# Spare blocks' expert weights: conditional plain transfers from SyncE in place of indirect loads from GpSimd

## What is computed

```python
gates = jnp.einsum('tk,tke->te', w, jax.nn.one_hot(idx, N_EXPERTS, dtype=F32))
def expert(acc, p):
    e_g, e_u, e_d, g = p                       # (1024,256), (1024,256), (256,1024), (T,)
    a = jax.nn.silu(t @ e_g) * (t @ e_u)
    return acc + g[:, None] * (a @ e_d).astype(F32), None
routed, _ = lax.scan(expert, jnp.zeros(t.shape, F32), (wg, wu, wd, gates.T))
```

## Time and profile before

| | us |
|---|---|
| median of 3 runs (lowest to highest) | 1770.37 (1769.48 to 1772.65) |
| profiled execution, span | 1780.7 |
| PE matmul busy | 1625.1 |
| DVE busy | 960.2 |
| POOL busy | 697.5 |
| ACT busy | 238.9 |

### The profile page before, as it was taken

How to read it: one execution, slowest core, us unless ns; L and a number is a source line. 1 busy time by engine, 2 the same in 40 slices (tenths; PEclk the granted TensorE clock), 3 DMA queues, 4 the chain that set the end, 5 groups by cost and what they waited for, 6 DMA issues and landing times.

```text
span 1780.7 us, 27338 instructions
## 1 busy us (share of the span) xinstructions
PE 1625.1 (91%) x10621; PEld 911.0 (51%) x10621; DVE 960.2 (54%) x2404; ACT 238.9 (13%) x607; POOL 697.5 (39%) x755
## 2 busy tenths in 40 slices
PE   7898998999799999999879989899999999999894
PEld 4674774444344444444367547644444444444443
DVE  3887467544345544444469663764444444444346
ACT  3223331000002100000031333100000000000001
POOL 1306006554454454544102240355445454545420
PEclk9998999999999999999989979999999999999997
DMA  9668475999999999999965765499999999999973
GB/s 324 226 238 289 147 281 220 413 372 339 403 410 384 366 403 409 401 373 383 370 232 189 261 241 215 179 365 407 384 383 414 402 389 394 414 387 388 397 280 150
DMA packets 185918, 588.83 MB, mean 331 GB/s; under 512 B 67705, under 2 KB 85837, under 8 KB 131902
## 3 DMA queue, kind: packets, MB, share of 16 engines
q1 hardware_dynamic: 115504, 506.99, 72.8%
q0 software_dynamic: 67232, 79.73, 13.0%
q10 hardware_dynamic: 3054, 0.38, 0.2%
HBM read 775.22 MB, written 56.95 MB: 467 GB/s over the span
## 4 chain that ended last, share of the span: by engine, by line
PE 60%; another core or an unknown queue 19%; DVE 9%; issue 4%; DMA 4%; ACT 3%; SPq 0%; POOL 0%; DVEq 0%; ACTq 0%; POOLq 0%
PE ps L1447 29%; PE ps L1460 9%; PE ps L1149 4%; PE ps L980 4%; PE ps L1295 3%; PE ps L1036 2%; ACT scratch L1745 2%; DMA raw<-in_exp_w_up,idx_w 2%; PE ps L1013 1%; PE ps L1044 1%; DMA ypart<-yrows_k 1%; PE ps L1438 1%; DVE scratch L2125 1%; DMA yrows_k<-ytok,idx_y 1%
## 5 line engine op out<-in xcount | busy, mean ns | idle before, releaser
L1447 PE MATMUL ps<-raw,xTs 128*64 128x256 f32 x6144 | 746.0, 394 | 5.3 <-DMA raw<-in_exp_w_up,idx_w 3.6
L1447 PEld LDWEIGHTS ps<-raw,xTs 128*64 128x64 f32 x6144 | 416.9, 136 | 267.1 <-issue 12.0
L927 POOL DMA_INDIRECT yrows_k<-ytok,idx_y x192 | 197.1, 1027 | 501.1 <-DVE ytok L2131 472.2
L1460 PE MATMUL ps<-dn,scratch 128*64 128x512 f32 x1536 | 364.7, 595 | 18.9 <-issue 17.2
L2246 DVE STREAM_TRANSPOSE xTs<-xg 64x256 f32<-64x256 f32 x768 | 335.7, 437 | 8.9 <-DMA xg<-hrows,idx_x 1.1
L2125 DVE TENSOR_TENSOR scratch<-scratch,ps 128x128 f32<-128x128 f32 x192 | 55.2, 287 | 434.7 <-ACT scratch L1745 361.9
L920 POOL DMA_INDIRECT xg<-hrows,idx_x x192 | 199.0, 1036 | 103.6 <-issue 57.1
L2131 DVE COPY ytok<-ps 128x512 f32<-128x512 f32 x192 | 132.3, 689 | 168.8 <-PE ps L1460 145.0
L1745 ACT ACTIVATE scratch<-ps 128x128 f32<-128x128 f32 x192 | 53.2, 277 | 1122.2 <-PE ps L1447 692.9
L1460 PEld LDWEIGHTS ps<-dn,scratch 128*64 128x64 f32 x1536 | 107.9, 136 | 167.3 <-issue 134.7
L980 PEld LDWEIGHTS ps<-cst,scratch 128*128 128x128 f32 x224 | 31.0, 141 | 216.0 <-issue 111.6
(11 more groups left out here) (394 smaller groups left out, 1296.3 us busy)
## 6 DMA issues: line engine op xcount, KB each, us to landing
raw<-in_exp_w_gate SPq DMA_DIRECT2D x128, 1024.0 KB
raw<-in_exp_w_up SPq DMA_DIRECT2D x128, 1024.0 KB
dn<-in_exp_w_down SPq DMA_DIRECT2D x128, 1024.0 KB
narrow<-in_w_ada SPq DMA_DIRECT2D x18, 1024.0 KB, 8.7
wide<-in_w_in SPq DMA_DIRECT2D x16, 1024.0 KB, 7.5
wide<-in_w_ada SPq DMA_DIRECT2D x16, 1024.0 KB, 8.8
ypart<-yrows_k SPq DMA_DIRECT2D x16, 1024.0 KB, 9.1
raw<-in_w_ada SPq DMA_DIRECT2D x14, 1024.0 KB, 17.0
```

The lines of the kernel that those rows point to most:

```text
L927: pool.indirect_dma_start(yrows_k.rearrange("t (h d) -> (t h) d", h=2), bass.IndirectOffsetOnAxis(ap=idx_y[:, b:b + 1], axis=0), ytok[n % ...
L1447: ins = mm(ps[64 * h:64 * h + 64, 2 + n % 2, 0:256], xTs[n % 2][:, k, :, :].rearrange("p u i -> p (u i)"), w[:, k, h], start=k == 0, stop= ...
L1460: ins = mm(ps[64 * h:64 * h + 64, 5 + n % 2, :], actT[:, n % 2, 64 * j:64 * j + 64], dn[n % NDOWN][:, j, 512 * h:512 * h + 512], start=j = ...
```

## The change

Spare blocks' weights are now issued by SP, in the same slots of the rings and with the same semaphores. For each spare block, `spare_expert` reads two numbers from SBUF into registers, the expert (`spare_of`) and whether the block is used (`spare_used`); the transfer's source address is made from the first, and with the second at 0 the whole transfer is skipped while its semaphore still goes up. The two numbers are read once for gate and up and once more for down. GpSimd's indirect weight loads and the table `idx_w` are gone; DVE writes two small tables in place of one. SP's order has the waits of the spare steps in it, and the first five steps of a layer are written out by hand, with step 2 last.

```diff
-    idx_w = placed("idx_w", "prodm", 0, [P, SPARE], U32)
+    spare_of = placed("spare_of", "prodm", 0, [P, SPARE], I32)
+    spare_used = placed("spare_used", "decS", BLOCKS, [P, SPARE], I32)
...
+            def spare_expert(b):
+                spare[0] = sp.value_load(spare_of[0:1, b - NE:b - NE + 1], min_val=0, max_val=NE - 1)
+                spare[1] = sp.value_load(spare_used[0:1, b - NE:b - NE + 1], min_val=0, max_val=1)
+
+            def expert(name, b):
+                v = a[name].rearrange("l e (p k) n -> (l e) p (k n)", p=P)
+                if b < NE:
+                    return v[NE * layer + b], None
+                return v[NE * layer + spare[0]], spare[1]
...
                 elif n == 2:
                     sp.wait_ge(out_first_used.sem, out_first_used.by(layer, 1))
+                    sp.wait_ge(spare_ready.sem, spare_ready.by(layer, 1))
...
+                loaded = raw_loaded[n % NRAW].sem
+                if b >= NE:
+                    spare_expert(b)
+                    loaded = spare_raw[SPARE_STEPS.index(n) % 2].sem
                 for j, name in enumerate(("exp_w_gate", "exp_w_up")):
-                    sp.dma_start(raw[n % NRAW][:, j], a[name][layer, b].rearrange("(p k) n -> p (k n)", p=P))\
-                        .then_inc(raw_loaded[n % NRAW].sem, 16)
+                    src, used = expert(name, b)
+                    sp.dma_start(raw[n % NRAW][:, j], src, cond=used).then_inc(loaded, 16)
...
-            for n in range(NSTEP + 2):
-                if n < NSTEP and STEPS[n] < NE:
+            gate_up(0)
+            gate_up(1)
...
+            down(0)
+            gate_up(3)
+            down(1)
+            gate_up(4)
+            down(3)
+            gate_up(2)
+            down(2)
+            for n in range(NRAW, NSTEP + 2):
+                if n < NSTEP:
                     gate_up(n)
-                if n >= 2 and STEPS[n - 2] < NE:
+                if n - 2 >= NDOWN:
                     down(n - 2)
...
-            for j, name in enumerate(("exp_w_gate", "exp_w_up")):
-                spare_weights(name, raw[2][:, j], 2, spare_raw)
...
-                m = n + NRAW
-                if m < NSTEP and STEPS[m] >= NE:
-                    pool.wait_ge(gu_made.sem, gu_made.by(layer, n + 1))
-                    for j, name in enumerate(("exp_w_gate", "exp_w_up")):
-                        spare_weights(name, raw[m % NRAW][:, j], m, spare_raw)
...
-                m = n - 1 + NDOWN
-                if n >= 1 and m < NSTEP and STEPS[m] >= NE:
-                    spare_weights("exp_w_down", dn[m % NDOWN][:, :, :].rearrange("p j n -> p (j n)"), m, spare_down)
```

More of the change, by code:

```diff
@@ L128 @@
 K_DST = K_SPARE + NE
-K_ROW = K_DST + 3 * TOPK
-K_Y = K_ROW + DEPTH
+K_Y = K_DST + 3 * TOPK
 K_SUM = K_Y + 1
@@ L359, in program @@
     raw = [placed(f"raw{n}", of, first, [P, 2, SEG], F32) for n, (of, first) in enumerate(raw_at)]
+    raw[2] = wide[:, 0]
     down_at = [("narrow", 0), ("mixT", 0), ("narrow", SEG), ("hT", 0)]
     dn = [placed(f"dn{n}", of, first, [P, 2, D], F32) for n, (of, first) in enumerate(down_at)]
+    dn[2] = narrow[:, 1].rearrange("p (j n) -> p j n", j=2)
     xg = [placed(f"xg{n}", "cosT", 512 * n, [P, 512], F32) if n < 4 else
@@ L701, in _ @@
                 sp.dma_start(seg(wide[:, 1, j]), a[name][layer].rearrange("(k p) n -> p k n", p=P)).then_inc(wide_loaded[1], 16)
+            spare = [None, None]
+            def spare_expert(b):
[6 more added lines that the diff above has]
+                return v[NE * layer + spare[0]], spare[1]
             def gate_up(n):
@@ L733, in down @@
                     sp.wait_ge(down_made.sem, down_made.by(layer, n - NDOWN + 1))
-                sp.dma_start(dn[n % NDOWN][:, :, :].rearrange("p j n -> p (j n)"),
-                             a["exp_w_down"][layer, b].rearrange("(p j) n -> p (j n)", p=P))\
-                    .then_inc(down_loaded[n % NDOWN].sem, 16)
-            for n in range(NSTEP + 2):
-                if n < NSTEP and STEPS[n] < NE:
-                    gate_up(n)
-                if n == 1:
-                    sp.wait_ge(out_made.sem, out_made.by(layer, 2 * (OUT_SEGS - 1)))
-                    sp.dma_start(narrow[:, 1].rearrange("p (k n) -> p k n", k=2),
-                                 a["shared_w_down"][layer].rearrange("(k p) n -> p k n", p=P)).then_inc(narrow_loaded[1], 16)
-                if n >= 2 and STEPS[n - 2] < NE:
+                loaded = down_loaded[n % NDOWN].sem
+                if b >= NE:
+                    spare_expert(b)
+                    loaded = spare_down[SPARE_STEPS.index(n) % 2].sem
+                src, used = expert("exp_w_down", b)
+                sp.dma_start(dn[n % NDOWN][:, :, :].rearrange("p j n -> p (j n)"),
+                             src, cond=used).then_inc(loaded, 16)
+            gate_up(0)
+            gate_up(1)
+            sp.wait_ge(out_made.sem, out_made.by(layer, 2 * (OUT_SEGS - 1)))
+            sp.dma_start(narrow[:, 1].rearrange("p (k n) -> p k n", k=2),
+                         a["shared_w_down"][layer].rearrange("(k p) n -> p k n", p=P)).then_inc(narrow_loaded[1], 16)
+            down(0)
[7 more added lines that the diff above has]
+                if n < NSTEP:
+                    gate_up(n)
+                if n - 2 >= NDOWN:
                     down(n - 2)
@@ L2236, in _ @@
             chain(v.tensor_reduce(spare_e, spare_is, AX.X, ALU.add))
-            ts(idx_w[:, :], spare_e, float(P), cst[:, K_ROW + layer:K_ROW + layer + 1], ALU.mult, ALU.add)\
-                .then_inc(spare_ready.sem, 1)
+            ts(spare_of[:, :], spare_e, float(NE - 1), None, ALU.min)
+            ts(spare_used[:, :], spare_e, float(NE), None, ALU.is_lt).then_inc(spare_ready.sem, 1)
             def turn_x(n):
```

12 lines of the change are left out of this document (removed).

## The result

The kernel after takes 1747.03 us (median of 4 runs, 1743.89 to 1748.27), the kernel before beside it 1769.92 (1764.23 to 1772.65). The ratio is 0.9876, 95% interval 0.9861 to 0.9892: 22.9 us faster, half of the 46 that I forecast. The span of the profiled execution is 1746.3.

The account below looks back on a forecast made before the run. Late semaphores behind GpSimd's long runs of indirect DMAs were taken to hold PE back, with DMA no steady-state bound. Terms: 49.3 - 8 + 2 + 7 = 50.3, less 4, gain 46, median 1724 us, range 1708 to 1746.

Parts of the forecast that it names:

- main term: Steady rounds of both mixtures: shorter GpSimd runs end late semaphores, 0.88 us in 28 rounds a layer, 49.3 us in all.
- DMA is no bound in the steady state: Steady rounds: DMA takes what the rings ask for; a round needs 16.7 us at 408 GB/s against 17.25 for PE.
- DMA rival: Mixtures: DMA becomes the bound if a round needs 17.1 us; 1742 us, chance 0.17.
- First steps: Start of each layer: three fewer loads in GpSimd's run gain 1 us a layer, bounds 0 and 3.
- First layer's DMA-starved stretch: First layer, steps 19 to 37: DMA-bound, so the 0.88 a round is not gained there; 8 us off.
- Used blocks: Used spare blocks: loads in SP's order win back 7 of 10 us; 4 subtracted for their DMA time.
- Skipped rows: Empty spare blocks: without their 384 tiny packets each, DMA gains at most 0.3 us a round; only the margin is helped.
- SP: SP's queue: register loads and skipped transfers (0.4 us each) bring it to 6 us of 17.25 a round; costed at nothing.
- The base: Whole kernel: gain 46 taken off the profiled 1780.7, about 1735; its span is 10.3 above the median, so 1724.
- ACT's starts: Sign of being right: ACT's silu starts within 0.3 us of the modelled end of gate_up in every step.
- remote: Label in ACT's waits for gate_up's late semaphore; its disappearance was a sign of being right.
- the steps of 5.75: Sign of being right: in steady rounds all three steps take 5.75 us, where one took 6.64.

Follow-up runs that it names:

- e0: The unchanged kernel before, profiled a second time, on chip 2: 1766.11 us.
- b3: The unchanged kernel before, profiled a fourth time, on chip 1: 1769.99 us.
- g2: Kernel after, second layer's parameters fetched one a step from step 10, first spare block moved from step 8 to 2; chip 3: 1747.5 us, ratio 0.9835.
- g2b: The kernel of g2 run once more, on chip 4: 1745.6 us, ratio 0.9823.
- f2: Kernel after with a zero fill on GpSimd in place of each of e1's 96 empty indirect loads a layer; chip 3: 1746.81 us, ratio 0.9834.
- after5: The kernel after, unchanged, run once more as base on chip 1: 1748.69 us, ratio 0.989.
- b2: The unchanged kernel before, profiled a third time, on chip 3: 1772.66 us.
- e3: Kernel after with every spare block taken as empty, so used spare blocks' weights are left out; chip 2: 1708.55 us, ratio 0.9678.
- e4: Kernel before with all rows of the spare blocks' indirect loads out of bounds, loads still issued; chip 2: 1720.48 us, ratio 0.9747.
- g4: The kernel of g2b with gathers issued four steps ahead in place of eight; chip 4: 1734.41 us, ratio 0.9758.
- e1: Kernel after with all 96 indirect loads a layer back on GpSimd, every row out of bounds; chip 1: 1765.34 us, ratio 0.9985.
- f3b: Kernel after with 96 empty indirect loads a layer of 2 rows each in place of 128; chip 1, one run: 1755.71 us.

## Why the prediction was wrong, step by step

The step that failed is the main term: "A round loses 0.88 us ... 49.3 in all". On a chip without late semaphores there is nothing of it to win: e0 and b3, the unchanged kernel, lose none. On a chip with them the 0.88 does leave each round (in g2 and g2b, which have the change, the silu is at most 0.55 us late from step 1 on). But it is not the time it costs. The unchanged kernel shows that: 1767.7, 1765.8 and 1767.4 us on the chips without late semaphores, 1777.4 and 1776.7 on the others. Otherwise these chips are not slower: f2, which has no long runs, takes 1746.81 on such a one, and after5 1748.69 on the other sort. Gross, the lateness is 49 us in the rounds by my sum (0.88 in 56 rounds; 51 in b2) and 12 in the first steps; net it is 10. The other 50 are waits for weights that come forward as soon as the lateness is gone (turn's waits and waits for weights: 4.4 + 48.5 in e0, 62.1 + 5.8 in b2).

I had taken the wait that was seen as the time that would be won, because "DMA is no bound in the steady state". It was none only because PE lost 0.88 us a round, and the trace had signs against it: PE waits in `down` from step 72 of the first layer on and from step 78 of the second, which I had counted away with "PE waits for no weights over dozens of rounds". The row of 381 GB/s at a share of 0.99 was read as "takes what the rings ask for". In e3 that is so, with nothing to spare: 383 GB/s, share 0.98, no excess. A used block's 7.7 us can then be made up only at the difference to the 415 GB/s of the fullest round, and most of it becomes a stall.

The DMA rival (0.17) had the mechanism and nearly the number, 1742 for 1747. Its rule was right: bytes over rate, less what the rings hold ahead. That its number came so near is in part luck: it was set against a profile with late semaphores and a median from other runs, and its split by layers (20 for the second, 6 to 10 for the first) is 14.7 and 12.1 between b3 and after5, on one chip.

The other terms:

- *First steps*, 2 us: on the profile the forecast was made from, the excess of steps 0 and 1 was 5.7 us a layer and became 0.7 and -0.9, 11.6 in all. But the change did not win this, as the two profiles are from chips of different sorts: e0, unchanged, has -0.9 in both layers, and g2 and g2b, with the change but on chips with late semaphores, have 5.9 and 5.9, 6.8 and 4.4. Eight gathers and the two behind them are run enough. So the term is about 0 on either sort of chip.
- *First layer's DMA-starved stretch*, -8: right in sign. The first layer gained 16.8 and the second 21.1, a difference of 4 (2.6 between b3 and after5, on one chip), where the forecast had 12.
- *Used blocks*, +7 and -4: they cost 5.6 us each after the change, 39 in all, and 6.5 each before. With both terms I had them at almost nothing. The stall of 3.63 us is gone, and 6.3 us of waits stand in the same steps, 88 to 90.
- *Skipped rows*, "helps the margin, nothing else": in a kernel bound by the DMA engines this is most of the gain. The 0.3 us a round would be 19 us in 64 rounds; e4 less e3 gives 12, of the 19.0 us that the change is worth on chip 1, and the used blocks' plain transfers the rest. The packets were 432 for an empty block (144 a load in e4), not 384.
- *SP*: right to cost it at nothing. A skipped transfer holds it 0.07 to 0.09 us, not 0.4, and a register load 0.27 + 0.16. SP issues a step's gate and up at most 2.0 us after the slot is free, but for steps 24 to 34 of the first layer, where the parameters hold it up to 10.7 us, as forecast.
- *The base*: the profiled 1780.7 came with late semaphores, as did b2 on a chip whose runs span 1770 to 1784. I moved the gain to a median of 1770 without asking why the profile stood above it.

Of what was to show it right, ACT's starts, "remote", the steps of 5.75 and GpSimd's 196.5 us (697.5 to 501.0) came true, and the time did not. ACT's starts and the missing "remote" are no sign of the change: e0 has both without it. And where the change does take the wait away, they tell that it is gone, not what it had covered.

What the change is worth on a chip with late semaphores was not measured: the kernel after itself was run beside before only on chip 1 (19.0 there) and in the first comparison (22.9), whose chip is not recorded. f2, 31 us below before on chip 3, is no stand-in, as its fills also break up the row of gathers at a layer's start. An estimate: f2's 1746.81 and the 11 us that g4 won over g2b at that place give 1758, so a gain of about 19 there too.

Rule and row: the Trainium skill, "DMA: Bandwidth & Descriptors", Specifications, gives a limit of about 358 GB/s; rounds of 408 and 415 GB/s stand against it as a bound for this one core. The other rule of the Trainium skill, in "Issuing engines are not separate DMA queues" of the same page, has the right premise. All queues share 16 engines, and their time was the bound. But to save only sequencer time is not all that the change did: the same bytes took these engines 17 to 20 us less when they came in plain transfers. That rule of the Trainium skill is about where a transfer is issued, and here its kind changed too.

## What to carry to other kernels

A late wait is worth what is left of it when the next bound moves up. Before summing waits, ask what the DMA engines would need at the full speed of PE, and take a share near 1.0 as a bound until a stretch with a lower share is found. In a DMA-bound stretch count the engines' time (share times span) of each queue, not bytes: an indirect load whose rows are all out of bounds still costs some 0.06 us of the result (12 us for 192 in e4 less e3; e1 gives 0.09, but with up to 7 of its 17 us from another wait). And when the profiled execution stands off the median, profile it again before using its waits, and compare two kernels' waits only on one chip: here the wait of 0.88 us a round would have been gone from the second profile without the change too.

## What the runs showed of the hardware

- Other engines' semaphores come late behind runs of six to ten of GpSimd's indirect DMAs (0.3 us apart) on some chips: 0.88 and 1.0 us a round in two profiles of before, 5.3 us at a layer's start in g2 and up to 5.5 in g2b, behind ten gathers. With four gathers in a row it did not happen (g4). On two other chips the same runs, at the same places of a step, do nothing (0.05 us). What differs between the chips stays open.
- Small indirect DMAs were the worst there: with loads of 2 rows the silu was 2.5 us late (median) in every third step, against 2.0 in b2, and the kernel took 1824.37 us, on the other sort of chip 1755.71.
- What of an empty load costs time is only partly settled. Loads of 128 rows of 512 B left 32 packets each (6144 more in 192), those of 8 KB in e4 144 each (27648), and the first cost 17 us, the second 12. So it isn't the packets that the profile counts. With 2 rows and the same 32 packets it was 7 (f3b, one run), and there it was no DMA time: PE's unnamed waits in `down` are 22.9 us in it, 31.0 in after5, and its waits on DVE's copy, behind late scatters as in e1, 11.7 against 1.5.
